# A hybrid encoder layer on one NeuronCore: the chunk recurrence laid over all 128 partitions, with halves of weight pieces between its steps

## The reference, cut to what matters

```
gc = cumsum(g)                                   # per head, within the chunk
decay = exp(where(causal, gc_i - gc_j, -inf))
kb = k * beta
lower = (kb @ k.T) * decay * (1 - eye)           # 64 x 64 per head
tmat = inverse(lower + eye)
u, w = tmat @ (v * beta), tmat @ (kb * exp(gc))
qk = (q @ k.T) * decay;  qg = q * exp(gc);  kd = k * exp(g_last - gc)
def step(s, ...):                                # chunk after chunk, state s is 128 x 128 per head
    v_new = u - w @ s
    o = qg @ s + qk @ v_new
    s = s * exp(g_last) + kd.T @ v_new
```

## Time and profile before

| | |
|---|---|
| median of three runs | 5901.41 us (5883.3 to 5908.81) |
| profiled execution, its own time | 5900.7 us |
| its span, first to last instruction | 5898.9 us |
| mean granted TensorE clock | 0.971 of full |
| TensorE, VectorE, ScalarE, GpSimd busy | 96%, 35%, 13%, 48% of the span |

### The profile page before, as it was taken

The page is one execution under the profiler, slowest core; times in us unless marked ns, Lnnn a source line. Parts: engine busy times, 40 slices in busy tenths (PEclk is TensorE's granted clock), DMA queues, the critical chain, the costliest instruction groups (busy, mean ns, idle before and its releaser), DMA issues.

```text
span 5898.9 us, 103917 instructions
## 1 busy us (share of the span) xinstructions
PE 5682.6 (96%) x42614; PEld 5596.8 (95%) x42614; DVE 2079.9 (35%) x3009; ACT 754.0 (13%) x1547; POOL 2818.5 (48%) x1576
## 2 busy tenths in 40 slices
PE   7999999999999988899999999999999999999998
PEld 7998889999999978899999999999999999999997
DVE  6933222222242049968332222222222222222223
ACT  3310000110110010078200000000000000000000
POOL 3443333333455534433455555555555555555553
PEclk9999989898999989999999999999999999999999
DMA  2331112222334221245433222222222222222222
GB/s 102 93 95 58 57 57 69 70 68 71 103 119 152 97 76 60 77 144 183 161 120 107 91 99 91 99 91 99 91 91 99 91 99 91 99 91 99 91 91 82
DMA packets 229428, 564.01 MB, mean 96 GB/s; under 512 B 53521, under 2 KB 102929, under 8 KB 224017
## 3 DMA queue, kind: packets, MB, share of 16 engines
q1 hardware_dynamic: 229136, 559.46, 28.3%
HBM read 488.65 MB, written 70.74 MB: 95 GB/s over the span
## 4 chain that ended last, share of the span: by engine, by line
PE 88%; DVE 5%; issue 2%; ACT 1%; DMA 0%; POOL 0%; DVEq 0%; SPq 0%; ACTq 0%; POOLq 0%
PE ps L1452 79%; PE aux L1559 4%; PE aux L1720 2%; PE aux L1627 1%; PE aux L1471 1%; PE aux L1626 1%; DVE ti L1283 0%; DVE mrall L1284 0%; DVE sel L1327 0%; ACT pp L706 0%; DVE ti L1291 0%; PE aux L1571 0%; DVE tv L1280 0%; DVE nt L926 0%; DVE sel L1322 0%
## 5 line engine op out<-in xcount | busy, mean ns | idle before, releaser
L1452 PE MATMUL ps<-xh,wh 128*128 128x288 f32 x7968 | 2409.2, 302 | 36.3 <-DVE xl L931 34.1
L1452 PE MATMUL ps<-xl,wh 128*128 128x288 f32 x7968 | 2369.5, 297 | 2.1 <-issue 2.1
L1452 PE MATMUL ps<-xh,wl 128*128 128x288 f32 x7968 | 2360.5, 296 | 0.0
L555 POOL CAST wh<-wr 128x1024 fp32r<-128x1024 f32 x786 | 838.7, 1067 | 2975.5 <-PE ps L1452 1685.6
L557 POOL TENSOR_TENSOR wl<-wr,wh 128x1024 fp32r<-128x1024 f32 x786 | 1979.6, 2519 | 63.0
L1452 PEld LDWEIGHTS ps<-xh,wh 128*128 128x128 f32 x7968 | 1513.2, 190 | 50.3 <-issue 30.5
L1452 PEld LDWEIGHTS ps<-xl,wh 128*128 128x128 f32 x7968 | 1515.8, 190 | 4.6 <-issue 2.7
L1452 PEld LDWEIGHTS ps<-xh,wl 128*128 128x128 f32 x7968 | 1518.0, 191 | 0.0
L1452 PE MATMUL ps<-yh,wh 128*128 128x288 f32 x4608 | 1374.7, 298 | 9.7 <-issue 5.0
L1452 PE MATMUL ps<-yl,wh 128*128 128x288 f32 x4608 | 1366.7, 297 | 0.0
L1452 PE MATMUL ps<-yh,wl 128*128 128x288 f32 x4608 | 1362.0, 296 | 0.0
(11 more groups left out here) (223 smaller groups left out, 2783.8 us busy)
## 6 DMA issues: line engine op xcount, KB each, us to landing
wr<-in_w SPq DMA_DIRECT2D x786, 512.0 KB, 3.3
gates_s<-gbuf SPq DMA_DIRECT2D x12, 3072.0 KB, 11.8
gtile<-gates_s SPq DMA_DIRECT2D x32, 1152.0 KB, 5.8
qkv<-qkv_s SPq DMA_DIRECT2D x9, 768.0 KB, 5.0
hid_s<-gl SPq DMA_DIRECT2D x20, 288.0 KB, 11.8
gl<-hid_s SPq DMA_DIRECT2D x20, 288.0 KB, 4.1
mg<-in_x SPq DMA_DIRECT2D x4, 1152.0 KB, 11.5
qkv_s<-lo SPq DMA_DIRECT2D x16, 288.0 KB, 3.0
```

Source lines behind the costliest of these rows:

```text
L555: pool.tensor_copy(wh[u][:, :, :], wr[u][:, :, :]).then_inc(S["hi_done"], 1)
L1452: mm_ = pe.matmul(ps[slot][:, half, 0:HT], a[w][:, t, :], b[:, k, cols], start=first and t == tiles_[0] and x == 0, stop=last and t == til ...
```

## The change: what it does

Even heads are kept on partitions 0 to 63 and odd heads on 64 to 127. The 64 x 512 tiles become 128 x 256, the 64 x 1024 tiles 128 x 512, and the per-position factors 128 x 36. TensorE's per-head products read and write the half that their head lies on. The layout takes these edits:
- ones2 and upper2, made once, are 128 x 128 with a 64 x 64 block for each half; gcb is one product with ones2 (256 columns), and two more products with plain ones give egb, one per half.
- xx is turned by per-head products with an identity, not by transposes; v and k are transposed two heads at once, 4 transposes in place of 8.
- The output and the state update of even and odd heads go to different PSUM banks.
- The raw factors (bar) are copied out twice, in eight operations; Sigmoid and Exp run once per half.

The order of the work changes as well:
- The k k^T and k q^T products come first in a chunk, before gcb, and VectorE forms the next chunk's lm (`decays(n + 1)`) right behind the state add, ahead of its fills 10 and 11.
- Fills 0 and 1 stand together before the transposes of xx and v; fill 2 behind these. At each level l the piece 2 + l is cut in two halves of 24 matmuls, one between p and z and one behind z. Fill 8 follows ks, fill 9 follows vn, and fills 10 and 11 follow the state update.

```diff
@@ VectorE
+        def decays(n):
+            dve.tensor_tensor(heads(lm[:, :]), per_token("gtok", n), per_mask(const("upper")), ALU.mult
+                              ).then_inc(S["gu_done"], 1)
         def delta(n, kind, i):
-            dve.tensor_tensor(heads(lm[:, :]), per_token("gtok", n), per_mask(const("upper", 64)), ALU.mult
-                              ).then_inc(S["gu_done"], 1)
+            if first:
+                decays(0)
...
             fill(0, kind, i)
+            fill(1, kind, i)
...
-                fill((3, 4, 6, 7, 8)[l - 1], kind, i)
+                fill(2 + l, kind, i)
...
+            fill(8, kind, i)
             fill(9, kind, i)
-            fill(10, kind, i)
             wait("sup_ps", n + 1)
...
+            if kind != "Z":
+                decays(n + 1)
+            fill(10, kind, i)
             fill(11, kind, i)
@@ TensorE
-        def fill(k, kind, i):
+        def fill(k, kind, i, part_of=None):
...
+            if part_of is None:
+                piece(hp, k, slot, *data, NPIECE * part, part == 0, part == n - 1)
+            elif part_of == 0:
+                piece(hp, k, slot, *data, NPIECE * part, part == 0, False, range(0, NPIECE // 2), ())
+            else:
+                piece(hp, k, slot, *data, NPIECE * part + NPIECE // 2, False, part == n - 1, range(NPIECE // 2, NPIECE))
...
+            mine = lambda t: (lambda h: side(t, h % 2)[:, h // 2 * C:(h // 2 + 1) * C])
+            wide = lambda t: (lambda h: side(t, h % 2)[:, h // 2, :])
+            narrow_out = lambda b, part: mine(quads(b, part))
-            pe_wait(S["gu_done"], n + 1)
-            if not first:
-                pe_wait(S["r_done"], n)
-            pe.matmul(aux[:, 1, :], const("ones", 64), lm[:, :], start=True, stop=True).then_inc(S["gcb_ps"], 1)
             pe_wait(S["chunk_in"], 16 * n + 16)
             if not first:
+                pe_wait(S["r_done"], n)
                 pe_wait(S["s_done"], n)
                 pe_wait(S["o_copied"], n)
-            per_head(bank(2), k_h, q_h)
-            per_head(bank(0), k_h, k_h).then_inc(S["kq_ps"], 1)
+            per_head(narrow_out(0, 1), k_h, q_h)
+            per_head(narrow_out(0, 0), k_h, k_h).then_inc(S["kq_ps"], 1)
+            pe_wait(S["gu_done"], n + 1)
+            pe.matmul(quads(1, 0), ones2[:, :], lm[:, :], start=True, stop=True).then_inc(S["gcb_ps"], 1)
+            for g in range(2):
+                last = pe.matmul(quads(2 + g, 0), side(const("ones"), g), side(lm, g), start=True, stop=True)
+            last.then_inc(S["egb_ps"], 1)
             fill(0, kind, i)
+            fill(1, kind, i)
             pe_wait(S["x1_done"], n + 1)
...
-                if l == 3:
-                    fill(5, kind, i)
+                fill(2 + l, kind, i, 0)
                 pe_wait(S["p_copied"], 5 * n + l)
-                last = per_head(bank(3), sq_h(xx), sq_h(pp))
+                last = per_head(narrow_out(3, 0), mine(xx), mine(pp))
                 if l < LEVELS - 1:
-                    last = per_head(bank(2), sq_h(pp), sq_h(xx))
+                    last = per_head(narrow_out(2, 1), mine(pp), mine(xx))
                 last.then_inc(S["z_ps"], 1)
-                fill((3, 4, 6, 7, 8)[l - 1], kind, i)
+                fill(2 + l, kind, i, 1)
...
             for h in range(H):
+                out = aux[:, h % 2, h // 2 * C:(h // 2 + 1) * C]
+                pe.matmul(out, state[:, h, :], qg[:, h * C:(h + 1) * C], start=True, stop=False)
+                last = pe.matmul(out, wide(vb)(h), mine(att)(h), start=False, stop=True)
             last.then_inc(S["o_ps"], 1)
-            per_head(wide(2, 128), lambda h: kd[:, h, :], lambda h: vb[:, h, :]).then_inc(S["sup_ps"], 1)
+            per_head(lambda h: fours(2 + h % 2)[:, h // 2, :], wide(kd), wide(vb)).then_inc(S["sup_ps"], 1)
+            fill(10, kind, i)
             fill(11, kind, i)
```

More of the change, by code:

```diff
@@ L30 @@
 HC = H * C
+HQ = H // 2
+PC = HQ * C
+PN = NCH * HQ
 SCW, SC_TAPS = 1024, 3
@@ L177, in trunk_program @@
     sdec = m.take("sdec", [128, H, 128])
[L178 to L183, removed]
+    vb = m.take("vb", [128, HQ, 128])
+    kd = m.take("kd", [128, HQ, 128])
+    rr = m.take("rr", [128, HQ, 128])
+    el = m.take("el", [128, PC])
+    ll = m.take("ll", [128, PC])
+    att = m.take("att", [128, PC])
+    upper2 = m.take("upper2", [128, 128])
+    ones2 = m.take("ones2", [128, 128])
     m = Region(r.pos, end)
@@ L652, in _ @@
             act.wait_ge(S[f"kept_qk{u}"], 16 * H)
-        act.activation(heads(small["beta"][:, :], H), raw_tok[:, :, 0:H], ACT.Sigmoid).then_inc(S["beta_done"], 1)
-        act.activation(decay[:, :], vector("alog")[0:64, :], ACT.Exp).then_inc(S["decay_exp"], 1)
+        for g in range(2):
+            act.activation(heads(side(small["beta"], g), HQ), side(raw_tok, g)[:, :, g:H:2], ACT.Sigmoid
+                           ).then_inc(S["beta_done"], 1)
+            act.activation(side(decay, g), side(vector("alog"), g)[:, g:H:2], ACT.Exp).then_inc(S["decay_exp"], 1)
         act.wait_ge(S["sp_in"], 1)
@@ L659, in _ @@
         act.wait_ge(S["gc_ps"], 1)
-        act.activation(small["eg"][:, :], aux[0:64, 0, 0:NCH * H], ACT.Exp)
-        act.activation(egl[:, :], aux[:, 1, 0:NCH * H], ACT.Exp).then_inc(S["eg_done"], 1)
-        act.wait_ge(S["kdec_in"], 1)
+        act.activation(small["eg"][:, :], aux[:, 0, 0:PN], ACT.Exp)
+        for g in range(2):
+            last = act.activation(heads(egl[:, :], H)[:, :, g:H:2], heads(aux[:, 1 + g, 0:PN], HQ), ACT.Exp)
+        last.then_inc(S["eg_done"], 1)
+        act.wait_ge(S["kdec_in"], 2)
         act.activation(small["kdec"][:, :], small["kdec"][:, :], ACT.Exp).then_inc(S["kdec_done"], 1)
@@ L1004, in _ @@
         wait("tok_ps", 1)
[L1005 to L1009, removed]
+        wait("beta_done", 2)
+        for g in range(2):
+            dve.tensor_tensor(heads(side(small["sp1"], g), HQ), side(raw_tok, g)[:, :, 32 + g:32 + H:2],
+                              side(vector("dtb"), g)[:, g:H:2].unsqueeze(1).to_broadcast([64, NCH, HQ]), ALU.add
+                              ).then_inc(S["sp_max"], 1)
+        dve.memset(upper2[:, :], 0.0).then_inc(S["sp_max"], 1)
+        dve.memset(ones2[:, :], 0.0).then_inc(S["sp_max"], 1)
+        wait("sp_max", 4)
+        for g in range(2):
+            dve.tensor_copy(side(upper2, g)[:, C * g:C * (g + 1)], side(const("upper"), g)).then_inc(S["pair_set"], 1)
+            dve.memset(side(ones2, g)[:, C * g:C * (g + 1)], 1.0).then_inc(S["pair_set"], 1)
         dve.tensor_scalar(sp2, sp1, -1.0, None, ALU.mult).then_inc(S["sp_max"], 1)
-        wait("sp_max", 2)
+        wait("sp_max", 5)
         dve.tensor_tensor(sp2, sp2, sp1, ALU.max).then_inc(S["sp_in"], 1)
@@ L1513, in _ @@
         for n in range(NCH):
-            last = pe.transpose(raw_flat[:, n * C:(n + 1) * C], bar[0:64, n * C:(n + 1) * C],
+            last = pe.transpose(raw_flat[:, n * C:(n + 1) * C], bar[0:64, n, :, :].rearrange("p g c -> p (g c)"),
                                 const("ident", 64)[:, 0:64])
@@ L1517, in _ @@
         pe.wait_ge(S["g_ready"], 1)
[L1518 to L1521, removed]
+        pe.wait_ge(S["pair_set"], 4)
+        pe.matmul(aux[:, 0, 0:PN], upper2[:, :], small["gtok"][:, :], start=True, stop=True)
+        for g in range(2):
+            last = pe.matmul(aux[:, 1 + g, 0:PN], side(const("ones"), g), side(small["gtok"], g),
+                             start=True, stop=True)
+        last.then_inc(S["gc_ps"], 1)
+        pe.wait_ge(S["kdec_in"], 2)
         pe.wait_ge(S["eg_done"], 1)
@@ L1546, in fill @@
                 data, n = (xh, xl), 2
[L1547 to L1552, removed]
+            if part_of != 1:
+                if part == 0:
+                    pe.wait_ge(S[f"evacuated{slot}"], ev)
+                if kind == "C" and k == 2:
+                    pe.wait_ge(S["sc_lo"], NSC)
+                pe.wait_ge(S["lo_done"], 2 * hp + k + 1)
+            if part_of is None:
[4 more added lines that the diff above has]
+                piece(hp, k, slot, *data, NPIECE * part + NPIECE // 2, False, part == n - 1, range(NPIECE // 2, NPIECE))
         def delta(n, kind, i):
@@ L1578, in delta @@
+            for g in range(2):
+                last = pe.matmul(quads(2 + g, 0), side(const("ones"), g), side(lm, g), start=True, stop=True)
+            last.then_inc(S["egb_ps"], 1)
             fill(0, kind, i)
+            fill(1, kind, i)
             pe_wait(S["x1_done"], n + 1)
-            for h in range(H):
-                last = pe.transpose(aux[0:64, 3, h * C:(h + 1) * C], xx[:, h * C:(h + 1) * C],
-                                    const("ident", 64)[:, 0:64])
-            last.then_inc(S["xt_ps"], 1)
+            per_head(narrow_out(1, 1), mine(xx), lambda h: side(const("ident"), h % 2)[:, C * (h % 2):C * (h % 2 + 1)]
+                     ).then_inc(S["xt_ps"], 1)
@@ L1584, in delta @@
             pe_wait(S["exp_done"], 3 * n + 3)
-            for h in range(H):
```

(13 more changed lines are left out.)

158 lines of the change are left out of this document (87 added, 71 removed).

## The result

The changed kernel takes 5710.45 us (median of four runs, 5709.0 to 5714.71) against 5901.16 us for the kernel before: ratio 0.9682, 95% interval 0.966 to 0.9705. I had forecast 5826, with 5775 to 5870 as the range. The direction was right; the gain is 191 us, where I had summed 75.

The account below looks back on a forecast made before the run. TensorE, busy 5682.6 of 5898.9 us, was taken to bound the kernel, so only time between weight pieces could be gained. Nine chunks -81, start +2, loop ends +4 gave -75: 5826 us, range 5775 to 5870.

Parts of the forecast that it names:

- each per-head product keeps its 16 instructions: Levels of a chunk: z1 to z4 stay at 2.0 us, the other four p at 1.07, z5 at 1.1; 13.4 in sum.
- (a): Rival, chance 0.17: tiles overlap where streaming bounds (ks, vn, update, egb), 33 us more, 5793; p near 0.6 exceeds it.
- halve, some 6 us per chunk: p and z of a chunk, if matmuls on different row groups run concurrently and issue does not limit them.
- the output's 7.3: The o pairs of a chunk still alternate a 128x128 with a 64-row weight, so their 7.3 us stays.
- the update's 3.52: State update's time before the change; 1.76 if two tiles run at once, and the middle, 2.6 us, was forecast.
- my 116.05: Forecast length in us of one new chunk, summed from its parts; nine are 1044.5, 81.0 less than before.
- The boundary: Between chunks: key products first, 3.65 us, the 5.1 us lm wait goes; B chunks gain 13.7, C chunks 5.4.
- The clock: Small-matmul stretches up to 2.0 us keep full clock; boundary loses it about every second time, 1.5 us; behind update 1.2.
- The new wait for short_out: Piece 6, behind p4, waits for its buffer to be freed: 0.2 us in four chunks, 0.1 on average.
- The idle at the ends of loops: TensorE may miss instructions at the three ends of loops in the stage: +4 us.
- The start: Stage start, once: extra copies, table loads and memsets against key products 4.4 us earlier, at half clock (+1.0); +2.0 in all.
- Rival (c): Chance 0.09: neighbours on different tiles do not overlap weight load and matmul; 161 us slower, 5987, or 6149 at full difference.

Follow-up runs that it names:

- experiment 1: Changed kernel with each per-head product running over the even heads first, then the odd ones: 5766.21 us, 0.9771 of the kernel before.
- experiment 2: Kernel before, on its old 64-partition layout, with only the new order of the work (key products first, early lm, half pieces, new fill places): 5816.33 us, 0.986.
- experiment 8: Kernel before with one edit, the output running over all eight state products, then all eight vb products: 5837.52 us, 0.9893.
- experiment 5: Changed kernel with lm formed late again, at the start of its own chunk behind VectorE's fills 10 and 11: 5728.92 us, 0.9711 of the kernel before.
- experiment 4: Changed kernel with whole pieces behind z and nothing between p and z at each level: 5726.38 us, 0.9711 of the kernel before.
- experiment 7: Changed kernel with the output running over all eight state products, then all eight vb products: 5662.67 us, 0.9597 of the kernel before.
- experiment 6: Changed kernel with per-head products in head order 0, 2, 1, 3, 4, 6, 5, 7: 5722.52 us (two runs), 0.9696 of the kernel before.

## Why the prediction was wrong, point by point

The step that failed is the bound I put on the per-head products: "each per-head product keeps its 16 instructions", hence its time. From the equal 62.5 ns of 64x64 and 128x64 weights I took issue as the limit. The step of 0.06 us in each of two series at once (experiment 1) shows it is a limit of one tile. p at 0.61 was my own sign for "more than (a)". The Trainium skill ("TensorE: Matmul & The Clock Gate", Part 3) had it right that matmuls on different row groups run concurrently; its 62 ns of issue per MATMUL ("Back-to-back issue gap") does not bind here, with 34 ns measured. I had left out its condition: the same row of that table gives 62 ns for hardware decode off, and about 25 ns as the floor otherwise, which 34 ns does not undercut. Which decode this chip ran, no run here shows. I had written down what overlap alone would give, "halve, some 6 us per chunk", and gave it no rival of its own; (a) held only 33 us of it and stopped at 5793.

| per chunk, us | predicted | order alone | changed |
|---|---|---|---|
| key products, gcb, egb | 3.65 | 3.1 | 2.3 |
| xT with vT; p1 with kT | 3.2 | 3.6 | 2.4 |
| z1 to z4, p2 to p5, z5 | 13.4 | 13.4 | 7.4 |
| ks, vn | 3.8 | 3.8 | 2.0 |
| output | 7.3 | 5.9 | 5.6 |
| state update | 2.6 | 3.5 | 1.4 |
| lost clock behind the update and at the boundary | 2.7 | 1.2 | 1.1 |
| wait for short_out in B chunks | 0.1 | 0 | 0.5 |

The last column is chunk 1 by its chain (102.0 us), the middle one chunk 2 of experiment 2 (113.7). Of 14 us that I had too much, 6.0 are p and z of the levels, 5.1 the other products and the transposes that gained (boundary 1.3, transposes 0.8, ks and vn 1.8, update 1.2), 1.7 the output, which ran at full clock in this chunk, and 1.6 the clock; 0.4 went the other way, to the wait for short_out. The average of the nine is 103.6 us (932.11 / 9), so 12.5 too much: what the overlap gave is the same in all chunks but for the start of chunk 0, while output and update average 6.4 and 1.7 us.

A second error is hidden in the output's 7.3 and the update's 3.52. Both were read from rows that ran partly or wholly at half clock, as this stretch within chunk 2's output of the kernel before shows, and I counted neither as lost clock:

```profile
776.00:778.00 2.00, 2.00 (x8) 0.50 0.28 74
```

At full clock the output takes 5.6 us on either layout, and the update on the old one takes 1.84 (experiment 8), near the 1.76 that I had put down for two tiles at once.

- The order: right. Experiment 2 gives 86 us for my 75. That its chunks average my 116.05 is luck in part, as terms were off both ways: update 3.3 to 3.5 against 2.6, output 5.6 to 7.1 against 7.3. What the order removes is the wait for lm (18 us in experiment 5), the waits for pp (16 in experiment 4) and slow pieces.
- The boundary: right in direction, not in size. I had asked for 13.7 us in a B chunk against 5.4 in a C chunk. Chunks 1 to 3 (B) gained 27.7, 24.8 and 23.1 us, chunks 5 to 7 (C) 21.3, 18.7 and 24.8. The B chunks gained 3.6 more on average, where I had 8, and the best C chunk as much as a B chunk. So the test that I had set for the boundary was passed only on average; and since the large common part falls out of a difference, it could not have shown the error in the products.
- The clock: between the pieces of the levels "no stretch of 2.0 us loses it" held in every run. The boundary, which I let lose it every second time, never slowed the pieces behind it in the changed kernel, but for the start of chunk 0. The 3.1 us of experiment 2 lost it once, in chunk 4, where 2.47 us of idle at a loop's end stand in the middle (15.49 for the two pieces). Length alone does not decide: 3.7 us (experiment 7) and 5.5 us (six chunks of experiment 8) kept the full clock, while the output's pairs lost it in five chunks of the changed kernel, in chunk 2 within 3 us of their start. What does decide stays open.
- The new wait for short_out came in four chunks, 1.8 us in all, 0.45 each in place of 0.2. The idle at the ends of loops was 3.7 us, against the 4 that I had.
- The start: from bar's first copy to the first key product of chunk 0 it takes 13.8 us, against 13.5 before; I had +1.0. The further table loads are there; the early key products pay for them.
- Rival (c) is out, and what it stood on was misread. Pairs of 181 ns are not the price of changing the tile's place. Sorted by size the same instructions cost 2.77 us on the new layout and 3.66 on the old (experiments 7 and 8), which fits a price on changing the size, with the second cause named in experiment 7 still open. The change of place costs nothing and gains (experiments 1 and 6). The rule of the Trainium skill ("TensorEngine Tiling (Array Packing)", Restrictions and Gotchas) on row tiles and one PSUM bank does not slow p and z, which write the lower and upper partitions of one bank at 34 ns each. Two row tiles into one bank on the same partitions wasn't tried.

Open: over how many instructions TensorE overlaps the two halves, beyond the four points of experiment 6; and 4.1 us by which the part after the stage is longer in the profiled execution (4362.4 against 4358.3), with 2.4 less ahead of the stage, where the very first norm product already starts 2.3 us earlier.

## What to carry to other kernels

Where small matmuls use half of the rows or half of the columns, try neighbours on different halves, one by one, before the waits between them: here the layout brought 138 us, the order 86. Where products on tiles of different size alternate, try them sorted by size, which was worth 62 us on the old layout and 48 on the new. A pace that several shapes share says nothing about which resource sets it, so such a limit belongs into the range from both sides.

## What the hardware showed that I had not expected

- Two 64x64 float32 products run side by side at 62 ns each, 34 per instruction; alternating columns alone (kq, 128 rows) gains as much, 2.01 to 1.08 us, and so does alternating rows without columns (vb and state update, 128 columns; the PSUM banks alternate, too), 1.93 to 1.04 and 1.84 to 0.95.
- With a change between 128x128 and 64x128 weights at every second instruction 32 instructions take 5.6 us at full clock; sorted, 2.77.
- Without those pairs the clock stayed at full through 3.7 us of small matmuls in all nine chunks, and the two pieces behind them took 12.99.
